# A hybrid decoder block in one kernel: last norm's weight row loaded earlier, and adds of the last output tiles put ahead of the scalings of the tile in front of them

## The reference

```python
h = rms_norm(x, norm_mix_g[i]); proj = h @ w_in[i]
...
x = x + jnp.concatenate([u, att, y], axis=-1) @ w_out[i]      # u: conv, att: attention, y: state space
h = rms_norm(x, norm_ffn_g[i])                                # the last norm
f = causal_dwconv(h @ w_up[i], ffn_conv_w[i], ffn_conv_b[i])
fa, fg = jnp.split(f, 2, axis=-1)
x = x + (jax.nn.silu(fg) * fa) @ w_down[i]
```

## Time and profile before

| | |
|---|---|
| median of 3 runs | 758.7 us |
| the profiled execution | 761.17 us |
| its span in the profile | 759.5 us |
| PE busy | 725.6 us (96%) |
| DVE busy | 474.6 us (62%) |
| ACT busy | 333.8 us (44%) |
| POOL busy | 103.7 us (14%) |
| mean granted clock of PE | 0.988 |

### The profile page before, as it was taken

One profiled execution on the slowest core, in us unless ns is written; L12 is line 12 of the kernel. 1 busy time (PEld: TensorE's weight loads), 2 busy tenths in 40 slices (PEclk: granted clock), 3 DMA queues, 4 the chain that ended last, 5 costly groups with the idle time before them and its releaser, 6 DMA issues.

```text
span 759.5 us, 9584 instructions
## 1 busy us (share of the span) xinstructions
PE 725.6 (96%) x3490; PEld 583.3 (77%) x3494; DVE 474.6 (62%) x727; ACT 333.8 (44%) x502; POOL 103.7 (14%) x83
## 2 busy tenths in 40 slices
PE   4999988899899989999979999999999999999998
PEld 4768876677667768888869888888888888888886
DVE  5259899958999956666665565656565656211222
ACT  6345563778546564722445434443444343221120
POOL 2001468532000003333130000000000000000000
PEclk9999999999999999999999999999999999999999
DMA  8723113211111143022222433243324421323302
GB/s 261 238 73 112 56 57 92 75 56 57 56 56 56 57 166 110 20 94 56 84 56 56 112 110 91 74 110 110 85 80 110 110 93 73 117 106 110 111 1 110
DMA packets 78049, 69.48 MB, mean 91 GB/s; under 512 B 5816, under 2 KB 64536, under 8 KB 78016
## 3 DMA queue, kind: packets, MB, share of 16 engines
q1 hardware_dynamic: 77871, 68.51, 29.3%
q10 hardware_dynamic: 144, 0.52, 0.2%
HBM read 66.91 MB, written 2.12 MB: 91 GB/s over the span
## 4 chain that ended last, share of the span: by engine, by line
PE 71%; DVE 11%; issue 7%; POOL 5%; ACT 5%; DMA 1%; DVEq 0%; POOLq 0%; ACTq 0%
PE bank L1470 61%; DVE u_acc L582 3%; PE bank L1476 2%; POOL stats L741 2%; DVE w_lo L592 2%; POOL u_acc L761 2%; PE bank L1490 2%; DVE xbcT L1278 1%; ACT w_hi L836 1%; PE bank L1730 1%; PE bank L1704 1%; DVE prob L1257 1%; PE bank L1678 1%; POOL x2n L807 1%; ACT prob L951 1%
## 5 line engine op out<-in xcount | busy, mean ns | idle before, releaser
L1470 PE MATMUL bank<-h_hi,w_hi 128*128 128x512 f32 (+1 forms) x496 | 194.4, 392 | 1.1 <-DVE h_lo L1109 1.1
L1470 PE MATMUL bank<-h_lo,w_hi 128*128 128x512 f32 (+1 forms) x496 | 190.9, 385 | 0.0
L1470 PE MATMUL bank<-h_hi,w_lo 128*128 128x512 f32 (+1 forms) x496 | 190.8, 385 | 0.0
L592 DVE TENSOR_TENSOR w_lo<-w_raw,w_hi 128x2048 fp32r<-128x2048 f32 x34 | 80.7, 2372 | 80.7 <-ACT w_hi L836 80.6
L1470 PEld LDWEIGHTS bank<-h_hi,w_hi 128*128 128x128 f32 x496 | 94.3, 190 | 27.5 <-issue 9.8
L1470 PEld LDWEIGHTS bank<-h_hi,w_lo 128*128 128x128 f32 x496 | 94.1, 190 | 18.5
L1470 PEld LDWEIGHTS bank<-h_lo,w_hi 128*128 128x128 f32 x496 | 94.5, 191 | 17.4
L836 ACT ACTIVATE w_hi<-w_raw 128x2048 fp32r<-128x2048 f32 x34 | 64.9, 1910 | 82.2 <-PE bank L1470 80.3
L1431 DVE SCALAR_TENSOR_TENSOR f<-bank,prm,f 128x511 f32<-128x511 f32 x88 | 65.8, 748 | 51.2 <-ACT f L1078 44.9
L1078 ACT ACTIVATE f<-bank,prm 128x512 f32<-128x512 f32 x44 | 33.9, 770 | 95.3 <-PE bank L1470 95.3
L1470 PE MATMUL bank<-w_hi,g_hi 128*128 128x512 f32 x176 | 68.5, 389 | 0.0
(11 more groups left out here) (227 smaller groups left out, 1027.0 us busy)
## 6 DMA issues: line engine op xcount, KB each, us to landing
w_raw<-in_w_up SPq DMA_DIRECT2D x44, 512.0 KB, 4.6
w_raw<-in_w_in SPq DMA_DIRECT2D x34, 512.0 KB, 4.5
w_raw<-in_w_down SPq DMA_DIRECT2D x22, 512.0 KB, 4.2
w_raw<-in_w_out SPq DMA_DIRECT2D x12, 512.0 KB, 4.3
x_in<-in_x SPq DMA_DIRECT2D x4, 512.0 KB, 6.8
tbias<-distance_table SPq DMA_DIRECT2D x1, 2048.0 KB, 8.2
x<-in_x SPq DMA_DIRECT2D x4, 512.0 KB, 6.5
out_x<-y_out SPq DMA_DIRECT2D x8, 256.0 KB, 2.0
```

What stands on the lines that cost most here:

```text
L592: eng.tensor_tensor(wlo[:, slot, cols], wraw[:, slot, cols], whi[:, slot, cols].bitcast(F32), ALU.subtract).then_inc(ready, 1)
L1470: ins = pe.matmul(o, a, b, start=first and i == 0 and q == 0, stop=last and i == n - 1 and q == 2)
```

## The change

Two things change.

First, `gf_row` moves to the address of tiles 0 and 1 of `xs_tok`, and SP issues its load at step ("seg", 2), after a wait for POOL's sixth count on `xd_ready`, in place of at ("ssdT", 3).

Second, the end of the plan is written anew: ("lo", 23) stands one slot earlier, ("wo", "ssm", 1, t) stands ahead of ("norm2", t - 1) for t = 1 and 2, both ("h2", 0) and ("h2", 1) stand ahead of the last quarter of chunk 22, and in the tail the add of the last tile comes after ("norm2", 2) and ("h2ev", 1).

```diff
-        fill[4 * c - 3].append(("lo", c))
+        fill[4 * c - (3 if c < UP0 else 4)].append(("lo", c))
...
-    for t in range(NT - 1):
-        put(last - 3 + t + 1, ("sq2", t, 1))
-        if t < NT - 2:
-            front[last - 3 + t + 2].append(("norm2", t))
-            put(last - 3 + t + 2, ("h2", t))
-            if t < NT - 3:
-                put(last - 3 + t + 3, ("h2ev", t))
+    put(last - 2, ("sq2", 0, 1))
+    put(last - 1, ("norm2", 0), ("sq2", 1, 1), ("h2", 0), ("h2", 1))
+    put(last, ("norm2", 1), ("sq2", 2, 1), ("h2ev", 0))
     return [step for parts in zip(front, slots, fill) for part in parts for step in part] + [
-        ("norm2", 2), ("wo", "ssm", 1, NT - 1), ("h2ev", 1), ("sq2", NT - 1, 1), ("h2", 2),
-        ("up0", 0, 0), ("h2ev", 2), ("norm2", 3), ("h2", 3), ("up0", 0, 1), ("h2ev", 3),
+        ("norm2", 2), ("h2", 2), ("h2ev", 1), ("wo", "ssm", 1, NT - 1), ("up0", 0, 0),
+        ("sq2", NT - 1, 1), ("norm2", 3), ("h2", 3), ("h2ev", 2), ("up0", 0, 1), ("h2ev", 3),
         ("up0", 1, 0), ("up0", 1, 1)]
...
-        gf_row = at("gf_row", [P, DM], F32, r5)
+        gf_row = at("gf_row", [P, DM], F32, r1 + 8 * K)
...
-                elif s == ("ssdT", NT - 1):
+                elif s == ("seg", 2):
 
-                    evacuated(sp, "yT", NT - 1)
+                    sp.wait_ge(xd_ready, 3 * 2)
                     sp.dma_start(gf_row[:, :], norm_ffn_g.to_broadcast([P, DM])).then_inc(s_gf, 16)
```

## The result

The changed kernel takes 753.62 us (median of 6 runs, 752.92 to 755.95), against 759.39 us for the kernel before (6 runs, 757.33 to 760.96: the three that gave 758.7 us, and three more). The ratio is 0.9929, with a 95% interval of 0.9906 to 0.9952: 0.7% faster, and an unchanged time lies outside the interval. I had said 753.4 us, 0.70% less. The profiled execution took 752.92 us, with a span of 751.2.

The account below looks back on a forecast made before the run. PE bounds the feed-forward part from 399.25 us; before it, PE's waits around the last norm count. Load 0, POOL 0, waits -4.0, clock -1.3 give -5.3 us: median 758.7 becomes 753.4 us, range 751.2 to 756.6.

Parts of the forecast that it names:

- The bound: Feed-forward part from 399.25 us: PE busy 357.06 of 357.15 us, so earlier there means earlier at the end.
- The load: Weight row on SP: issued after the instruction over at 321.0, there at about 327, 40 us before use; price 0.
- POOL's products: Four products with the weight row: POOL free at 377.7, before any power; one meets `w_lo` of chunk 22; price 0.
- The chain to tile 0: Last norm, tile 0: add 380.05, square 380.8, mean 381.5, scaling 382.45; PE's wait of 1.8 us gone.
- Tile 1: Before the last quarter of chunk 22: PE waits 1.0 us, turn possible at 385.55, products start at 386.4.
- The first lot: First 24 products of chunk 23: start at 390.2, not 394.22, 4.0 us earlier, after `h_lo` of tile 1.
- The clock: First 24 products of chunk 23: full clock taken, 2.95 us and not 4.24, 1.3 us more gained.
- The sum: Whole kernel: 0 (load) + 0 (POOL) - 4.0 (waits) - 1.3 (clock) = -5.3 us.
- the clock falls all the same: Rival around the last norm: the clock's 1.3 us stay lost, 4.0 us gained, 754.7 us; chance 0.15.
- slower: Rival: transposes and waiting at 383.7 bring the clock down, 1.7 us per fall, 763 or so; chance 0.03.
- Tile 1's turn comes later: Rival before the last quarter: 1 to 2 us more wait, gain 3.3 to 4.3, 754.4 to 755.4; chance 0.13.
- given back at chunk 24: Rival: weights of chunk 24 don't move along, all gain beyond 2.3 us is lost, 756.4 us; chance 0.07.

Follow-up runs that it names:

- load alone: The kernel before with only the early load and new address of the weight row, old plan order; 755.11 us, ratio to before 0.9955.
- order alone: The change with the weight row's load and address put back as before, new plan order kept; 757.60 us, ratio to before 0.9981.
- the four products on POOL: The change with four extra unused 128x512 products on POOL between the powers of tiles 0 and 1; 759.40 us, ratio to before 1.0009.
- two products more on POOL: The change with two extra unused 128x512 products on POOL between the powers of tiles 0 and 1; 754.35 us, ratio to before 0.9961.

## Why the prediction was right

- **The bound.** PE's 357 us from the second lot on are unchanged, so what came earlier there came earlier at the end. Right.
- **The load.** Predicted: the row is there long before it is used, at no cost. It was asked for at 318.2, 321.1 in the times of before, where I had 321.0. Right.
- **POOL's products.** Predicted: over before the first power, one lengthened beside `w_lo` of chunk 22. Right, 3.20 us. I had let `w_lo` grow to 3.08 as well; it took 2.28, since it had started first (below). That cost nothing either way.
- **The chain to tile 0.** Add, square, mean, scaling at 380.05, 380.8, 381.5 and 382.45. Measured, with 2.86 added: 380.02, 380.74, 381.49, 382.43. Right, and so was the wait of 1.8 us in front of tile 0 that went.
- **Tile 1.** Predicted: a wait of 1.0 us, turn at 385.55, last quarter at 386.4. Measured: 385.51 and 386.36, with 0.77 us of idle time named in the row and 0.95 from the end of tile 0's turn (380.85 + 0.85) to tile 1's. Right.
- **The first lot.** Predicted 390.2, measured 390.08, limited as I said by `h_lo` of tile 1, with tile 2's turn ending at the same moment.
- **The clock.** The one step that I took rather than worked out: full clock in the first lot, 1.3 us. It held in three profiles of three, and both profiles of before had the fall. The load alone keeps the clock too, though PE there still waits 1.65 and 1.02 us as it did before; the wait of 1.8 us in front of tile 0 is what it lacks. That this wait decides is argued, not shown. By the lowest times (before 4.0 us over the change, which is the waits without the 1.3) some executions of before may not have had the fall, so a part of this term may be luck of the two profiles. The other ground that I gave for a kept clock, that the longest stretch without products shrinks from 4.9 us to 2.7, does not hold as a reason: the load alone has one of 4.8 and kept the clock.
- **The sum.** 5.3 us predicted, 5.4 in the stretch, 5.8 between the medians; with the change and before measured twice more, 5.0 and 5.3. That 753.4 us was met within 0.2 owes something to the scatter: the medians of before lie between 758.3 and 759.4 us.

Of the rivals, "the clock falls all the same" and "slower" did not come true, but their mechanism is real: the order alone lost 2.8 us to it, and the four products on POOL 1.3. In single profiles it fell in a wait of 4.6 us, and in the second of two of 1.8 and 1.2; it didn't with one of 1.9, nor with the 1.65 and 1.02 of the load alone. The price that I took for a fall, 1.7 us from the one at 208 to 216 us, was misread: that one cost the kernel nothing, and those that cost something took 1.2 to 1.6, or 2.8 in the order alone. "Tile 1's turn comes later" did not, and nothing was given back at chunk 24. What the Trainium skill says of transposes (TensorE: Matmul & The Clock Gate, Part 4: PE-mode transpose), that they don't count as busy, fits the order alone, where PE did only 8 transposes and waited before the clock fell. It doesn't settle the matter: the load alone had 4.8 us of transposes and waits and no fall, and no run here takes transposes and waiting apart.

What I did not foresee is how the gain divides. By my sum the load and the order were one thing. Measured, the load alone gives 3.4 us, the order on top of it 2.05, and of this the adds' place 1.4, tile 1's turn 0.5 and the place of `w_lo` 0.4, each taken away alone (together 2.4, a little more than the 2.05 that they give at once). The new order of the tail was not taken away alone.

## What to carry to other kernels

A load that an off-path engine waits for is worth what stands behind that engine's next small instruction: here four products of POOL, and behind them the power for the norm. Where a chain goes over three engines, walk it tile by tile with the distances between starts that the trace has for an undisturbed tile; that gave times within 0.15 us. Put what the chain's next link needs ahead of work that only ends the link before, and fill an engine's wait inside the chain with half of a long instruction rather than put the whole in front.

## What the runs showed of the hardware

**An element-wise instruction of DVE with two inputs from SBUF and one of POOL shut each other out, whichever started first going on undisturbed.** In the change `w_lo` of chunk 22 started first, and only POOL's product grew:

```profile
364.86 2.28 DVE L588 TENSOR_TENSOR w_lo<-w_raw,w_hi 128x2048 fp32r<-128x2048 f32 x1
```

2.28 us, with 3.20 for the product, which starts at 365.08 and ends 1.14 behind the end of `w_lo`. Before, `w_lo` of chunk 23 started while a product was under way, and so both grew: `w_lo` to 3.08, and the product behind it to 3.32. With `w_lo` in its old slot it started at 377.27 and took 2.28; the power of one column, begun at 377.43, took 2.53 us in place of 0.55 and ended 0.4 behind it. With two products more on POOL, tile 0's scaling on DVE, whose inputs both lie in SBUF, started 0.07 us behind one of them and took 1.78 us in place of 0.75. An add out of PSUM, with one input from SBUF, lay beside a product in the change (370.29 to 370.98, the product from 369.57 to 370.87): the one took its 0.69 us, the other its 1.30. The Trainium skill says this (SBUF — State Buffer, Who interferes with whom): the pair of ports that the two engines share is an exclusive lock for the whole instruction. The trace agrees.

**The clock's falls cost nothing or 1.2 to 2.8 us, by where they come.** Near 100, 150 and 284 us each moved all that follows, by 1.2 to 1.6 us; near 130 and 208 us none did. Around the last norm one cost 1.3 us, and 2.8 in the order alone, where it lasted from before 386 to past 392 us. They come and go between executions of one kernel, so that two single profiles can differ by 2.9 us for no reason of the kernel's.
